# Modulation as columns, pair by pair, with the first row chunk normalised and multiplied in step with it

## The chip, the cores and the metric

The kernel runs on one NeuronCore of a Trainium2 chip. The metric is device time in microseconds, the median of several executions. One further execution was taken by the hardware profiler, and every row below comes from it. The engines are PE (TensorE: MATMUL, with its weight loads shown apart as PEld), DVE (VectorE), ACT (ScalarE), POOL (GpSimd) and SP (SyncE, which here only issues DMAs).

## What is computed

Two layers of a diffusion backbone over 1152 tokens of width 1024 (1024 sample tokens, 128 prompt tokens). Of a layer only its entry matters here:

```
mod_ctx = silu(c_ctx) @ w_mod[l] + b_mod[l]      # (3072,)
mod_lat = silu(c)     @ w_mod[l] + b_mod[l]
shift, scale, gate = split(mod, 3)
xn = rmsnorm(h, norm_g) * (1.0 + scale) + shift
a_in, a_z, b_in, b_z, q_lat, kv_lat, k_rope, c_z, g_all = split(xn @ w_in)
```

After it come the Fourier, pooling and attention branches, their gates, and the output projection with its residual.

## The kernel before, in words

Each engine has a program of its own, and semaphores join them. What follows is layer 0, up to the end of its token-major products.

**Modulation.** The shift and scale parts of `w_mod[0]` come as 16 units of 128 columns (`raw`, four slots of 128x8x128 floats, 512 KB a unit; unit n takes the slot of unit n-4 and so waits for its last use, `load_units`, L518). `mod_item` (L1562) multiplies a unit with PE: for each of 8 blocks of the contraction the stationary operand is `silu_c` (128x2, two conditions) and the unit's block moves past it, 128 columns. The result is a row pair, 2x128, which DVE copies to `mod_flat` (L1220). In the trace each float32 product is two weight loads and two matmuls, so an item is 16 of each. When all 16 are copied, 16 small transposes (L1591) turn them into columns, one DVE instruction adds the bias (L1222), and `scales` (L1208) forms the factors.

**Normalising.** The 9 row tiles of 128 tokens go in three chunks of 384 tokens. ACT squares and sums a tile (L700), takes the root (L705), DVE scales the rows (L1153, `xhat`). Then for each of 8 feature blocks f: three PE transposes (`norm_turn`, L1579, into PSUM banks 6 and 7), ACT applies scale and shift (`norm_values`, L718), DVE rounds to the high part (L1172), and the low part is a subtraction on POOL for even f (L987) and on DVE for odd f (L1175). ACT may be three blocks ahead of the low parts.

**Weights of the products.** Six units of `w_in` ("tok" 0 to 5) are split into high and low parts, ACT first (L685), POOL second (L980). Units 0 and 1 serve the products of kind p=0 (256 columns), units 2 to 5 those of kind p=1 (416 columns).

**Token-major products.** For p=0 and then p=1, for each of the 9 tiles, 8 blocks of three matmuls (`three_pass`, L1552 to L1554) into banks 0 to 2. ACT reads each result out (L750 for p=0, L753 and L754 for p=1). The turns of chunks 1 and 2 stand between the matmuls of tiles 1 and 4 of p=0. After the 18 tile products the feature-major products begin.

**Order.** SP issues six units, then a row tile and three units, three times over, then the rest of the units up to "tok" 1, three constants, and the later rows and units. All of layer 0's modulation stands ahead of the first turn on PE and ahead of the first value on ACT.

Of the kernel before, what the change touches and what calls it, by code (L numbers as in the profile page):

```python
# [107 lines left out]
def bank_plan():  # L108
# [48 lines left out]
NORM_IN_OUT = {5: (0, 0, 3), 6: (0, 3, 6), 7: (0, 6, 8)}  # L157
NORM_IN_ROWS = {1: 1, 4: 2}

# [102 lines left out]
def hybrid_step(nc, x_prompt, x_sample, cache_ckv, cache_krope, c, c_ctx, norm_g, w_mod, b_mod, w_in,  # L262
# [124 lines left out]
    vec_rows = r.put("vec_rows", [P])  # L387
    mod_flat = r.put("mod_flat", [16, P])

# [54 lines left out]
    def wcols(w, l, c0, width=P):  # L444
        return w[l].rearrange("(k p) n -> p k n", p=P)[:, :, c0:c0 + width]
    for m in range(16):
        unit(("mod", 0, m), [(0, KF, wcols(w_mod, 0, m * P))], None, (0, "mod", m))
    for l in range(DEPTH):
        for u, (c0, width) in enumerate(TOK_UNITS):
            split_unit(("tok", l, u), [(0, KF, wcols(w_in, l, c0, width))], 2 + u if u < 2 else 4 + u,  # L450
                       (l, "tok", (TT if u < 2 else 2 * TT) - 1))
        last_in[0] = (l, "tok", 2 * TT - 1)
# [104 lines left out]
    def _(sp):  # L557
# [13 lines left out]

        load_units(sp, 0, 6)
        for t in range(CT):
            load_rows(t)
            load_units(sp, 6 + 3 * t, 9 + 3 * t)
        load_units(sp, 15, unit_at[("tok", 0, 2)])
        for dst, src in ((q_scale, "q_scale"), (edge, "edge"), (pool_mat, "vec_zero")):
            sp.dma_start(dst[:], tab[src]).then_inc(S("const_in"), 16)
        for t in range(CT, 2 * CT):
            load_rows(t)  # L580
        load_units(sp, unit_at[("tok", 0, 2)], unit_at[("tok", 0, 4)])
        for t in range(2 * CT, TT):
            load_rows(t)
        for l in range(DEPTH):

            for ch in range(NCH):
                low_done(sp, KF * ((l * NCH) + ch + 1))
                sl = slice(ch * CH, (ch + 1) * CH)
                sp.dma_start(park_hi[:, :, sl], XH[:, :, sl].bitcast(F32)).then_inc(S("parked"), 16)
                sp.dma_start(park_lo[:, :, sl], XL[:, :, sl].bitcast(F32)).then_inc(S("parked"), 16)  # L590
                if ch == 0:
                    load_units(sp, unit_at[("tok", l, 4)], unit_at[("tok", l, 5)] + 1)
# [82 lines left out]
    def _(act):  # L675
# [31 lines left out]
        def norm_values(l, ch, f0, f1):  # L707

            for f in range(f0, f1):
                n = ch * KF + f  # L710
                b = filled(act, l, "norm", n)
                if n + l * NCH * KF >= 3:
                    low_done(act, l * NCH * KF + n - 2)
                if f == 0:
                    act.wait_ge(S("scale_ready"), l + 1)
# [18 lines left out]
        for l in range(DEPTH):  # L734

            filled(act, l, "norm", KF - 1)
            squares(l, 1)
            roots(l, 1)
            squares(l, 2, PS[:, 3:5, :].rearrange("p b n -> p (b n)"))
            roots(l, 2)  # L740
            for p in range(2):
                for t in range(TT):
                    b = filled(act, l, "tok", p * TT + t)
                    if t == 0:
                        act.wait_ge(S("xhat"), 9 * l + (9 if p else 3))
                        if l:
                            for ch in ((1, 2) if p else (0,)):
                                act.wait_ge(S(f"mid_out{ch}"), 16 * CT)
                    if p == 0:
                        ins = a.activation(atok[:, t, :], PS[:, b, 0:256], ACT.Copy)  # L750
                    else:
                        s = t if t < 8 else 9
                        a.activation(qlat[:, t, :], PS[:, b, 0:QR], ACT.Copy)  # L753
                        ins = a.activation(kvk[:, s, 0:LATENT - QR], PS[:, b, QR:LATENT], ACT.Copy)  # L754
                    ins.then_inc(bank_free[b], 1)
                    if p == 0 and t + 1 in NORM_IN_ROWS:
                        norm_values(l, NORM_IN_ROWS[t + 1], 0, KF)
                    if p == 0 and t in (2, 5):
                        for u in ((2, 3) if t == 2 else (4, 5)):
                            split_high(("tok", l, u))  # L760
                    if p == 1 and t in (3, 5):
                        split_high(("feat", l, t // 5))
            if l:
# [207 lines left out]
    def _(pool):  # L971
# [10 lines left out]
        def norm_low(l, ch, f0=0, f1=KF):  # L982
            for f in range(f0 + f0 % 2, f1, 2):
# [4 lines left out]
                                ALU.subtract).then_inc(S("xn_low_even"), 1)  # L988

        split_low(("tok", 0, 0))  # L990
        norm_low(0, 0, 0, 4)
        split_low(("tok", 0, 1))
        norm_low(0, 0, 4, KF)
        for l in range(DEPTH):
            for u in range(2, 6):
                if u % 2 == 0:
                    norm_low(l, u // 2)
                split_low(("tok", l, u))
            split_low(("feat", l, 0))
            split_low(("feat", l, 1))  # L1000
# [139 lines left out]
    def _(dve):  # L1140
# [73 lines left out]
        read_out(dve, 0, "vec", 0)  # L1214
        for m in range(16):
            if m == 10:
                norm_factors(0, 0)
                norm_rows(0)
            b = filled(dve, 0, "mod", m)
            v.tensor_copy(mod_flat[0:2, m, :], PS[0:2, b, 0:P]).then_inc(bank_free[b], 1)  # L1220
        b = filled(dve, 0, "modt", 0)
        v.tensor_tensor(modT[:, 0, 0:16, :], PS[:, b, 0:32].rearrange("p (m c) -> p m c", c=2),  # L1222
                        vecT[:, 0:16].unsqueeze(2).broadcast_to([P, 16, 2]), ALU.add).then_inc(bank_free[b], 1)
        read_out(dve, 0, "modt", 0)
        scales(0)
        norm_dve(0, 0)

        for l in range(DEPTH):

            norm_factors(l, 1)  # L1230
            norm_rows(1)
            norm_factors(l, 2)
            norm_dve(l, 1)
            norm_rows(2)
# [4 lines left out]
            for t in range(TT):  # L1239
                s = t if t < 8 else 9  # L1240
                read_out(dve, l, "tok", TT + t)
                squares = rot_tmp[:].rearrange("p a b -> p (a b)")
# [304 lines left out]
    def _(pe):  # L1547
# [7 lines left out]

        def mod_item(m):

            b = pe_takes(pe, 0, "mod", m)
            nu = unit_at[("mod", 0, m)]
# [25 lines left out]
        pe.wait_ge(S("silu_c"), 2)  # L1585
        for m in range(16):
            mod_item(m)
        for m in range(10, 16):
            read_out(pe, 0, "mod", m)
        for m in range(16):  # L1590
            ins = nc.tensor.transpose(PS[:, 6, 2 * m:2 * m + 2], mod_flat[0:2, m, :], ident[0:2, 0:2])  # L1591
        ins.then_inc(bank_full[6], 1)
        norm_turn(0, 0, 0, KF)

        for l in range(DEPTH):

            for p in range(2):
                pe.wait_ge(S("split_low"), split_k[("tok", l, 5 if p else 1)] + 1)
                for t in range(TT):
                    if p == 0 and t % CT == 0:  # L1600
                        low_done(pe, KF * (l * NCH + t // CT + 1))
                    b = pe_takes(pe, l, "tok", p * TT + t)
                    sl = slice(t * P, (t + 1) * P)
                    out = PS[:, b, 0:LATENT if p else 256]
                    for k in range(KF):
                        wh, wl = (wlat[:, i, k, :] if p else bs[:, 0:2, i, k, :] for i in range(2))
                        if p == 0 and t in NORM_IN_ROWS:
                            norm_turn(l, NORM_IN_ROWS[t], k, k + 1)
                        ins = three_pass(out, XH[:, k, sl], XL[:, k, sl], wh, wl, k == 0, k == KF - 1)
                    ins.then_inc(bank_full[b], 1)  # L1610

# [276 lines left out]
```

## Time and profile before

| | us |
|---|---|
| median of 3 runs | 2243.26 (2242.95 to 2243.73) |
| the profiled execution | 2243.49 |
| its span on the core | 2241.4 |
| PE busy | 2159.3 |
| DVE, ACT, POOL busy | 1088.0, 880.8, 650.6 |
| last read-out of a token-major product of layer 0 begins | 136.65 |

The span is the stretch that the profiler covers, and the profiled execution's own time is 2.1 us above it. A busy share is an average over the span. The change touches only the first part, so the stretches up to the last read-out are the ones to read.

### The profile page before, as it was taken

The page shows a single profiled execution, that of the slowest core. Times are in us where ns is not written, and L with a number is a line of the kernel's source. Part 1 is how long each engine was busy: PE and PEld are TensorE (multiplying, and loading weights), DVE is VectorE, ACT ScalarE, POOL GpSimd, SP SyncE. Part 2 cuts the span into 40 slices and gives each one's busy share as a digit, 9 for nine tenths or more (in the row PEclk, how much of TensorE's full clock was granted, in tenths as well). Part 3 has the DMA queues.
Part 4 walks back from the last instruction along what each step waited for, and adds up shares of the span by engine and source line. Part 5 has one row for each costly group of instructions (what it writes and reads, how often), then busy time and mean ns, then how long its engine had stood idle before and what let it go on. Part 6 is the DMA issues. An engine that isn't in the chain of part 4 may idle for free.

```text
span 2241.4 us, 36176 instructions
## 1 busy us (share of the span) xinstructions
PE 2159.3 (96%) x13453; PEld 2016.8 (90%) x13453; DVE 1088.0 (49%) x2773; ACT 880.8 (39%) x2203; POOL 650.6 (29%) x574
## 2 busy tenths in 40 slices
PE   6999999999989999999999999999999999999997
PEld 4999878878889999999989997778878999999997
DVE  3440368888845667663152314888886111120313
ACT  2421257777831212113152213777777112111312
POOL 1223022322321234333441321222323213343252
PEclk9999999999999999999999999999999999999999
DMA  9710000000343333224255100000005111111132
GB/s 286 255 34 25 26 1 1 1 1 1 120 145 92 94 83 99 72 66 135 68 201 169 33 8 25 1 1 2 1 2 202 48 36 48 42 50 42 45 132 85
DMA packets 194623, 155.69 MB, mean 69 GB/s; under 512 B 8637, under 2 KB 186001, under 8 KB 193425
## 3 DMA queue, kind: packets, MB, share of 16 engines
q1 hardware_dynamic: 194448, 153.38, 22.3%
q8 instruction: 108, 1.77, 0.3%
q14 instruction: 67, 0.54, 0.1%
HBM read 124.89 MB, written 28.48 MB: 68 GB/s over the span
## 4 chain that ended last, share of the span: by engine, by line
PE 84%; DVE 6%; ACT 4%; issue 3%; DMA 1%; SPq 0%; POOL 0%; DVEq 0%; POOLq 0%; ACTq 0%
PE ps L1552 22%; PE ps L1554 22%; PE ps L1553 22%; PE ps L1732 4%; PE ps L1686 3%; PE ps L1757 3%; PE ps L1758 2%; PE ps L1689 2%; DVE partmax L1399 1%; DVE kT L1369 1%; DVE probsT L1412 1%; DMA raw<-in_w_mod 1%; PE ps L1562 1%; ACT kT L857 1%; PE ps L1660 1%
## 5 line engine op out<-in xcount | busy, mean ns | idle before, releaser
L1552 PE MATMUL ps<-xn_high,split_ws 128*128 128x384 f32 x1488 | 499.6, 336 | 0.0
L1554 PE MATMUL ps<-xn_high,split_ws 128*128 128x384 f32 x1488 | 497.3, 334 | 0.0
L1553 PE MATMUL ps<-xn_low,split_ws 128*128 128x384 f32 x1488 | 497.1, 334 | 0.0
L938 ACT ACTIVATE sigmoids<-ps 128x384 f32<-128x384 f32 x144 | 70.5, 492 | 620.3 <-PE ps L1554 620.3
L1553 PEld LDWEIGHTS ps<-xn_low,split_ws 128*128 128x128 f32 x1488 | 279.5, 188 | 0.0
L1552 PEld LDWEIGHTS ps<-xn_high,split_ws 128*128 128x128 f32 x1488 | 279.4, 188 | 0.0
L1554 PEld LDWEIGHTS ps<-xn_high,split_ws 128*128 128x128 f32 x1488 | 279.3, 188 | 0.0
L1412 DVE TENSOR_TENSOR probsT<-ps,probsT 128x384 fp32r<-128x384 f32 x384 | 213.3, 555 | 70.6 <-ACT sum_inv_rows L833 41.1
L810 ACT ACTIVATE probs<-ps,negmax 128x384 f32<-128x384 f32 (+1 forms) x400 | 229.7, 575 | 20.0 <-DVE negmax L1405 19.5
L826 ACT ACTIVATE probsT<-ps 128x384 fp32r<-128x384 f32 x384 | 188.8, 492 | 83.3 <-PE ps L1732 52.3
L1732 PE MATMUL ps<-ident,probs 128*128 128x128 f32 x1168 | 198.0, 277 | 18.7 <-DVE kT L1369 15.0
L1399 DVE TENSOR_REDUCE partmax<-ps 128x1 f32<-128x384 f32 (+1 forms) x400 | 212.4, 535 | 1.7 <-PE ps L1554 1.3
L980 POOL TENSOR_TENSOR split_ws<-raw,split_ws 128x1024 fp32r<-128x1024 f32 x66 | 158.9, 2409 | 163.4 <-ACT split_ws L685 163.4
L1732 PEld LDWEIGHTS ps<-ident,probs 128*128 128x128 f32 x1168 | 132.4, 140 | 81.6 <-issue 74.6
L1489 DVE TENSOR_TENSOR products<-ps,sigmoids 128x384 f32<-128x384 f32 x96 | 53.5, 557 | 293.0 <-PE ps L1554 240.3
L1107 POOL TENSOR_TENSOR merged<-merged,products 128x384 f32<-128x384 f32 x90 | 92.3, 1026 | 334.7 <-DVE products L1489 333.9
L1757 PE MATMUL ps<-probsT,head_values 128*128 128x256 f32 x576 | 156.2, 291 | 12.4 <-DVE mixed_out L1433 12.4
L1552 PE MATMUL ps<-kT,qT 128*128 128x384 f32 (+1 forms) x400 | 163.2, 408 | 1.0 <-ACT probs L810 1.0
L1069 POOL TENSOR_TENSOR branch<-mixed_out,branch 64x256 f32<-64x256 f32 (+1 forms) x80 | 54.3, 679 | 338.8 <-DVE mixed_out L1433 337.9
L1758 PE MATMUL ps<-probsT,head_values 128*128 128x256 f32 x576 | 150.6, 281 | 0.0
L1554 PE MATMUL ps<-kT,qT 128*128 128x384 f32 (+1 forms) x400 | 134.1, 335 | 0.0
L1553 PE MATMUL ps<-kT,qT 128*128 128x384 f32 (+1 forms) x400 | 133.3, 333 | 0.0
(222 smaller groups left out, 4577.5 us busy)
## 6 DMA issues: line engine op xcount, KB each, us to landing
raw<-in_w_in SPq DMA_DIRECT2D x74, 512.0 KB, 4.0
raw<-in_w_mod SPq DMA_DIRECT2D x48, 512.0 KB, 5.2
park_high<-xn_high SPq DMA_DIRECT2D x6, 1536.0 KB, 6.7
park_low<-xn_low SPq DMA_DIRECT2D x6, 1536.0 KB, 10.6
xn_high<-park_high SPq DMA_DIRECT2D x2, 4608.0 KB, 16.2
rows<-in_x_sample SPq DMA_DIRECT2D x16, 512.0 KB, 6.7
raw<-in_w_out SPq DMA_DIRECT2D x16, 512.0 KB, 6.9
rows_mid<-rows SPq DMA_DIRECT2D x9, 512.0 KB, 2.6
```

The lines of the kernel that those rows point to most:

```text
L810: a.activation((P0, P1)[m % 2][:, c * CH:c * CH + w], PS[:, b, 0:w], ACT.Exp, bias=negmax[:, m % 2:m % 2 + 1], accum_out=partsum[:, m % 2, ...
L826: ins = a.activation(turned_place(m, gg, 0), PS[:, b, 0:n * P].rearrange("p (k c) -> p k c", k=n), ACT.Copy)
L980: g.tensor_tensor(d[:, 1], raw_unit(n), d[:, 0].bitcast(F32), ALU.subtract).then_inc(S("split_low"), 1)
L1107: g.tensor_tensor(Y[:, u % KF, sl], Y[:, u % KF, sl], prod[:, q % 2, :], ALU.add).then_inc(S("y_sum"), 1)
L1399: v.tensor_reduce(partmax[:, m % 2, c:c + 1], PS[:, b, 0:w], AX.X, ALU.max).then_inc(S("partmax"), 1)
L1412: v.tensor_tensor(turned_place(m, gg, 1), PS[:, b, 0:n * P].rearrange("p (k c) -> p k c", k=n), turned_place(m, gg, 0).bitcast(F32), ALU.s ...
L1552: mm(out, wh, xh, start=first, stop=False)
L1553: mm(out, wh, xl, start=False, stop=False)
L1554: return mm(out, wl, xh, start=False, stop=last)
L1732: ins = nc.tensor.transpose(PS[:, b, q * P:(q + 1) * P], (P0, P1)[m % 2][:, (3 * gg + q) * P:(3 * gg + q + 1) * P], ident[:])
L1757: mm(PS[:, b, 0:w], vhl, xh, start=(kt == 0 or gr == 4), stop=False)
L1758: ins = mm(PS[:, b, 0:w], vhl, xl, start=False, stop=last)
```

## The change

The kernel's text changes in five places.

- **Operands.** `mod_item` makes the unit's 128x128 block the stationary operand and lets the two columns of `silu_c` move, so that the result is a column pair, 128x2. DVE adds the bias from PSUM straight into `modT`. `mod_flat`, the 16 small transposes and `scales(0)` go.
- **Order of the items.** `MODS` takes shift f and scale f together. After each pair DVE forms the scale of block f, and `scale_ready` counts blocks.
- **Chunk 0 beside it.** From pair 3 on PE makes turns of chunk 0 behind the pairs (`TURN_IN_MODS`), and steps of the three p=0 tiles of chunk 0, block by block (`TOK_IN_MODS`, `tok_step`), with all three tiles open in banks 0 to 2. Chunk 1 follows in the same manner, two blocks behind its turns. The items have banks 3 to 5 instead of 0 to 5.
- **Order of the tiles.** In layer 0 three tiles of p=1 come after the six tiles of p=0, with the turns of chunk 2 in the second of them (`TOK_ORDER`, `NORM_IN_TOK`).
- **Loads.** The rows of chunk 0 come behind units 0 and 1 and behind units 2 and 3; "tok" 0 stands behind item 5 and "tok" 1 behind item 7 in the chain of slots. "tok" 2 to 5 come before the rows of chunk 2, the constants last.

```diff
-    add(0, "mod", 0, 6, 16)
-    add(0, "modt", 6, 1, 1)
+    add(0, "mod", 3, 3, 16)
...
+NORM_IN_TOK = ({(1, 1): 2}, {(0, 1): 1, (0, 4): 2})
+MODS = [m for f in range(KF) for m in (f, KF + f)]
+TOK_ORDER = ([(0, t) for t in range(2 * CT)] + [(1, t) for t in range(CT)] + [(0, t) for t in range(2 * CT, TT)]
+             + [(1, t) for t in range(CT, TT)],
...
+TURN_IN_MODS = {3: (0, 1), 4: (2, 3), 5: (4, 5), 6: (6,), 7: (7,)}
+TOK_IN_MODS = {5: (0,), 6: (1, 2), 7: (3, 4, 5, 6, 7)}
+DVE_IN_MODS = {3: (0,), 4: (1, 2), 5: (3, 4), 6: (5, 6), 7: (7,)}
...
+    for i, m in enumerate(MODS):
+        unit(("mod", 0, m), [(0, KF, wcols(w_mod, 0, m * P))], None, (0, "mod", i))
+        if i in (5, 7):
+            tok_unit(0, (i - 5) // 2)
...
+        load_units(sp, 0, 2)
+        load_rows(0)
+        load_rows(1)
+        load_units(sp, 2, 4)
+        load_rows(2)
+        load_units(sp, 4, unit_at[("tok", 0, 2)])
+        for t in range(CT, 2 * CT):
             load_rows(t)
+        load_units(sp, unit_at[("tok", 0, 2)], unit_at[("tok", 0, 5)] + 1)
+        for t in range(2 * CT, TT):
+            load_rows(t)
...
+                if l == 0 and ch == 0:
+                    act.wait_ge(S("scale_ready"), f + 1)
...
+        norm_values(0, 0, 0, 2)
         split_high(("tok", 0, 0))
-        norm_values(0, 0, 0, 4)
         split_high(("tok", 0, 1))
-        norm_values(0, 0, 4, KF)
+        norm_values(0, 0, 2, KF)
...
+            if l == 0:
+                for t in range(CT):
+                    tok_rows(0, t)
+                split_high(("tok", 0, 2))
+                split_high(("tok", 0, 3))
+                norm_values(0, 1, 0, KF)
+                split_high(("tok", 0, 4))
+                split_high(("tok", 0, 5))
+            squares(l, 2, beside_squares)
             roots(l, 2)
...
+        norm_low(0, 0, 0, 2)
         split_low(("tok", 0, 0))
-        norm_low(0, 0, 0, 4)
         split_low(("tok", 0, 1))
-        norm_low(0, 0, 4, KF)
+        norm_low(0, 0, 2, KF)
         for l in range(DEPTH):
             for u in range(2, 6):
-                if u % 2 == 0:
+                if l and u % 2 == 0:
                     norm_low(l, u // 2)
                 split_low(("tok", l, u))
+                if l == 0 and u % 2:
+                    norm_low(l, u // 2)
...
-                ins = mm(PS[0:2, b, 0:P], silu_c[:, k, :], raw[:, nu % 4, k, :], start=(k == 0), stop=(k == KF - 1))
+                ins = mm(PS[:, b, 0:2], raw[:, nu % 4, k, :], silu_c[:, k, :], start=(k == 0), stop=(k == KF - 1))
...
+        def tok_step(ch, k):
+
+            low_done(pe, KF * ch + k + 1)
+            for t in range(ch * CT, (ch + 1) * CT):
+                n = tok_item(0, 0, t)
+                b = pe_takes(pe, 0, "tok", n) if k == 0 else item(0, "tok", n)[0]
+                sl = slice(t * P, (t + 1) * P)
+                ins = three_pass(PS[:, b, 0:256], XH[:, k, sl], XL[:, k, sl], bs[:, 0:2, 0, k, :], bs[:, 0:2, 1, k, :],
+                                 k == 0, k == KF - 1)
+                if k == KF - 1:
+                    ins.then_inc(bank_full[b], 1)
+
+        for f in range(KF):
+            mod_item(2 * f)
+            mod_item(2 * f + 1)
+            for ff in TURN_IN_MODS.get(f, ()):
+                norm_turn(0, 0, ff, ff + 1)
+            for k in TOK_IN_MODS.get(f, ()):
+                if k == 0:
+                    pe.wait_ge(S("split_low"), split_k[("tok", 0, 1)] + 1)
+                tok_step(0, k)
+        for k in range(KF + 2):
+            if k < KF:
+                norm_turn(0, 1, k, k + 1)
+            if k >= 2:
+                tok_step(1, k - 2)
```

On PE, at the seam from the modulation to the first products, the program before has all items, the small transposes, all eight turns of chunk 0 and then tile 0:

```order
L1562 MATMUL ps<-raw,silu_c 2x128 x128
L1591 MATMUL ps<-ident,mod_flat 128x2 x16
L1579 MATMUL ps<-ident,xhat 128x128 x24
L1552 MATMUL ps<-split_br,xn_high 128x256
L1553 MATMUL ps<-split_br,xn_high 128x256
```

On PE, in the changed program, item 7, the turns of blocks 0 and 1, pair 4 (items 8 and 9) and the turn of block 2 read so; the output is now 128x2 and `raw` the stationary operand:

```order
L1599 MATMUL ps<-silu_c,raw 128x2 [waits raw_in0,bank_free4]
L1599 MATMUL ps<-silu_c,raw 128x2 x7
L1616 MATMUL ps<-ident,xhat 128x128 [waits bank_free6,xhat]
L1616 MATMUL ps<-ident,xhat 128x128 x5
L1599 MATMUL ps<-silu_c,raw 128x2 [waits raw_in2,bank_free5]
L1599 MATMUL ps<-silu_c,raw 128x2 x7
L1599 MATMUL ps<-silu_c,raw 128x2 [waits raw_in3,bank_free3]
L1599 MATMUL ps<-silu_c,raw 128x2 x7
L1616 MATMUL ps<-ident,xhat 128x128 [waits bank_free6]
L1616 MATMUL ps<-ident,xhat 128x128 x2
```

The turns of chunk 0 moved from behind all items to between them, beginning behind item 7.

On SP, in the DMA queue of the changed program from item 4's unit on, the units' loads and what each waits for:

```order
L533 DMA raw<-in_w_mod 128x8x128 [waits bank_full3]
L533 DMA raw<-in_w_mod 128x8x128 [waits bank_full4]
L533 DMA raw<-in_w_in 128x8x128 [waits bank_full5]
L533 DMA raw<-in_w_mod 128x8x128 [waits bank_full3]
L533 DMA raw<-in_w_mod 128x8x128 [waits bank_full4]
L533 DMA raw<-in_w_in 128x8x128 [waits bank_full5]
L533 DMA raw<-in_w_mod 128x8x128 [waits split_low]
L533 DMA raw<-in_w_mod 128x8x128 [waits bank_full3]
L533 DMA raw<-in_w_mod 128x8x128 [waits bank_full4]
L533 DMA raw<-in_w_mod 128x8x128 [waits split_low]
```

Item 8's unit (the seventh row, the first that waits for `split_low`) now stands behind the splitting of "tok" 0; before, every modulation unit waited for a PE product alone.

On ACT, in the changed program, between the two roots of chunks 1 and 2:

```order
L721 ACTIVATE root<-ssq 128x3 [waits mean_sq]
L762 ACTIVATE fourier_in<-ps 128x256 [waits xhat,bank_full0]
L762 ACTIVATE fourier_in<-ps 128x256 [waits bank_full1]
L762 ACTIVATE fourier_in<-ps 128x256 [waits bank_full2]
L701 ACTIVATE split_latent<-raw 128x8x128 [waits raw_in2]
L701 ACTIVATE split_latent<-raw 128x8x128 [waits raw_in3]
L736 ACTIVATE xn_value<-ps,modT,scaleT 128x384 [waits xn_low_odd,xn_low_even,bank_full6]
```

Before, the root of chunk 1 had only the squares of chunk 2 between itself and the root of chunk 2; the read-outs, the splits and all values of chunk 1 moved in between.

## Rows read from the trace of the kernel before

**Rows 1.** Page, busy us (share of the span) and instructions.
```profile
PE 2159.3 (96%) x13453; PEld 2016.8 (90%) x13453; DVE 1088.0 (49%) x2773; ACT 880.8 (39%) x2203; POOL 650.6 (29%) x574
```

**Rows 2.** Stretches: us, busy of PE, PEld, DVE, ACT, POOL, clock, DMA share, GB/s.
```profile
20.00:40.00 20.00, 16.26 (x146) 11.64 (x144) 3.52 (x10) 4.71 (x8) 0.00 (x0) 1.00 1.14 305
40.00:60.00 20.00, 11.89 (x76) 9.41 (x74) 14.71 (x26) 11.85 (x20) 9.05 (x6) 0.66 0.94 314
...
90.00:100.00 10.00, 10.00 (x73) 9.96 (x72) 0.00 (x0) 1.16 (x3) 1.69 (x2) 1.00 1.06 325
```

**Rows 3.** Waits of PE, 0 to 220 us: total, times, longest.
```profile
PE ps L1562 <- DMA raw<-in_w_mod: 6.2, 4, 2.5
...
PE ps L1552 <- DVE xn_low L1175: 5.0, 1, 5.0
```

**Rows 4.** Timeline, modulation items: start us, us, engine, what, count [idle before].
```profile
7.61 12.83 PE L1562 MATMUL ps<-raw,silu_c 128*2 128x128 f32 x96 [2.48 <-DMA raw<-in_w_mod]
11.29 0.28 DVE L1220 COPY mod_flat<-ps 2x128 f32<-2x128 f32 x1 [5.88 <-PE ps L1562]
...
35.14 7.15 PE L1562 MATMUL ps<-raw,silu_c 128*2 128x128 f32 x64 [1.26 <-DMA raw<-in_w_mod]
```

**Rows 5.** Weight loads by form (stationary width after the star), busy us, mean ns.
```profile
L1562 PEld LDWEIGHTS ps<-raw,silu_c 128*2 128x2 f32 x256 | 22.1, 88 | 15.0 <-issue 7.5
...
L1689 PEld LDWEIGHTS ps<-ckvT,wkv 128*64 128x64 f32 x96 | 9.3, 135 | 10.6 <-DVE kT L1369 3.0 <-ACT spectrum L799 1.4 <-issue 0.5
...
L1707 PEld LDWEIGHTS ps<-spectrum,chan_dft 128*128 128x128 f32 x32 | 5.2, 192 | 1.9 <-issue 1.9
```

**Rows 6.** Timeline of PE, single matmuls whose starts give the spacing.
```profile
57.57 0.42 PE L1554 MATMUL ps<-split_br,xn_low 128*128 128x256 f32 x1
57.78 0.41 PE L1552 MATMUL ps<-split_br,xn_high 128*128 128x256 f32 x1
...
337.09 0.28 PE L1553 MATMUL ps<-kT,qT 128*128 128x128 f32 x1
337.21 0.28 PE L1554 MATMUL ps<-kT,qT 128*128 128x128 f32 x1
```

**Rows 7.** Timeline of PE, small transposes and turns (three per turn).
```profile
42.76 1.12 PE L1591 MATMUL ps<-ident,mod_flat 2*128 2x2 f32 x16 [0.46 <-DVE mod_flat L1220]
...
64.10 0.49 PE L1579 MATMUL ps<-ident,xhat 128*128 128x128 f32 x3
...
64.79 0.49 PE L1579 MATMUL ps<-ident,xhat 128*128 128x128 f32 x3
```

**Rows 8.** Stretches of PE alone: us, busy, granted clock, DMA share, GB/s.
```profile
44.00:46.00 2.00, 0.85 (x6) 1.00 1.02 363
48.00:50.00 2.00, 1.68 (x7) 0.50 1.08 350
60.00:61.00 1.00, 1.00 (x11) 1.00 1.04 372
```

**Rows 9.** Timeline and chain: one value, two splits, a first load, a square.
```profile
3.44 4.03 DMA raw<-in_w_mod
...
42.19 1.06 ACT L685 ACTIVATE split_br<-raw 128x1024 fp32r<-128x1024 f32 x1 [4.22 <-DMA raw<-in_w_in]
43.33 2.35 POOL L980 TENSOR_TENSOR split_br<-raw,split_br 128x1024 fp32r<-128x1024 f32 x1 [42.88 <-ACT split_br L685]
...
51.35 0.67 ACT L718 ACTIVATE xn_value<-ps,modT,scaleT 128x384 f32<-128x384 f32 x1 [0.38 <-PE ps L1579]
...
58.51 1.03 ACT L700 ACTIVATE ps<-rows 128x1024 f32<-128x1024 f32 x1
```

**Rows 10.** Timeline of ACT, read-outs of tile products.
```profile
92.95 0.38 ACT L750 ACTIVATE fourier_in<-ps 128x256 f32<-128x256 f32 x1 [2.50 <-PE ps L1554]
95.83 0.39 ACT L750 ACTIVATE fourier_in<-ps 128x256 f32<-128x256 f32 x1 [2.50 <-PE ps L1554]
...
132.12 0.39 ACT L753 ACTIVATE qlat<-ps 128x256 f32<-128x256 f32 x1 [3.96 <-PE ps L1554]
136.65 0.39 ACT L753 ACTIVATE qlat<-ps 128x256 f32<-128x256 f32 x1 [3.96 <-PE ps L1554]
```

More of the change, by code:

```diff
@@ L728, in _, with tok_rows @@
         roots(0, 0)
+        norm_values(0, 0, 0, 2)
         split_high(("tok", 0, 0))
-        norm_values(0, 0, 0, 4)
         split_high(("tok", 0, 1))
-        norm_values(0, 0, 4, KF)
+        norm_values(0, 0, 2, KF)
         for l in range(DEPTH):
+            def tok_rows(p, t):
+                b = filled(act, l, "tok", tok_item(l, p, t))
+                if t % CT == 0:
+                    act.wait_ge(S("xhat"), 9 * l + (3 if p == 0 else 6 if l == 0 and t == 0 else 9))
+                if l and t == 0:
+                    for ch in ((1, 2) if p else (0,)):
+                        act.wait_ge(S(f"mid_out{ch}"), 16 * CT)
+                if p == 0:
+                    ins = a.activation(atok[:, t, :], PS[:, b, 0:256], ACT.Copy)
+                else:
+                    s = t if t < 8 else 9
+                    a.activation(qlat[:, t, :], PS[:, b, 0:QR], ACT.Copy)
+                    ins = a.activation(kvk[:, s, 0:LATENT - QR], PS[:, b, QR:LATENT], ACT.Copy)
+                ins.then_inc(bank_free[b], 1)
+            beside_squares = PS[:, 3:5, :].rearrange("p b n -> p (b n)")
             filled(act, l, "norm", KF - 1)
@@ L738, in _ @@
             roots(l, 1)
-            squares(l, 2, PS[:, 3:5, :].rearrange("p b n -> p (b n)"))
-            roots(l, 2)
[L741 to L762, printed above, removed]
+            if l == 0:
[7 more added lines that the diff above has]
+            squares(l, 2, beside_squares)
+            roots(l, 2)
+            for p, t in TOK_ORDER[l][CT if l == 0 else 0:]:
+                tok_rows(p, t)
+                if (p, t + 1) in NORM_IN_TOK[l]:
+                    norm_values(l, NORM_IN_TOK[l][p, t + 1], 0, KF)
+                if l and p == 0 and t in (2, 5):
+                    for u in ((2, 3) if t == 2 else (4, 5)):
+                        split_high(("tok", l, u))
+                if p == 1 and t in (3, 5):
+                    split_high(("feat", l, t // 5))
             if l:
@@ L1214, in _ @@
         read_out(dve, 0, "vec", 0)
-        for m in range(16):
-            if m == 10:
+        for f in range(KF):
+            if f == 3:
                 norm_factors(0, 0)
                 norm_rows(0)
[L1219 to L1226, printed above, removed]
+            for i in (2 * f, 2 * f + 1):
+                m = MODS[i]
+                b = filled(dve, 0, "mod", i)
+                v.tensor_tensor(modT[:, 0, m, :], PS[:, b, 0:2], vecT[:, m:m + 1].broadcast_to([P, 2]), ALU.add)\
+                    .then_inc(bank_free[b], 1)
+            read_out(dve, 0, "mod", 2 * f + 1)
+            v.tensor_scalar(scaleT[:, f, :], modT[:, 0, KF + f, :], 1.0, vecT[:, 48 + f:49 + f], ALU.add, ALU.mult)\
+                .then_inc(S("scale_ready"), 1)
+            for ff in DVE_IN_MODS.get(f, ()):
+                norm_dve(0, 0, ff, ff + 1)
         for l in range(DEPTH):
@@ L1231, in _ @@
             norm_rows(1)
-            norm_factors(l, 2)
-            norm_dve(l, 1)
+            if l == 0:
+                norm_dve(l, 1)
+                norm_factors(l, 2)
+            else:
+                norm_factors(l, 2)
+                norm_dve(l, 1)
             norm_rows(2)
@@ L1240, in _ @@
                 s = t if t < 8 else 9
-                read_out(dve, l, "tok", TT + t)
+                read_out(dve, l, "tok", tok_item(l, 1, t))
                 squares = rot_tmp[:].rearrange("p a b -> p (a b)")
@@ L1585, in _ @@
         pe.wait_ge(S("silu_c"), 2)
[L1586 to L1593, printed above, removed]
-        for l in range(DEPTH):
[L1597 to L1610, printed above, removed]
@@ new lines, in _ @@
+        for f in range(KF):
+            mod_item(2 * f)
[11 more added lines that the diff above has]
+                tok_step(1, k - 2)
@@ new lines, in _ @@
+        for l in range(DEPTH):
+            for p, t in TOK_ORDER[l][2 * CT if l == 0 else 0:]:
+                if t == 0:
+                    pe.wait_ge(S("split_low"), split_k[("tok", l, 5 if p else 1)] + 1)
+                if p == 0 and t % CT == 0:
+                    low_done(pe, KF * (l * NCH + t // CT + 1))
+                n = tok_item(l, p, t)
+                b = pe_takes(pe, l, "tok", n)
+                sl = slice(t * P, (t + 1) * P)
+                out = PS[:, b, 0:LATENT if p else 256]
+                for k in range(KF):
+                    wh, wl = (wlat[:, i, k, :] if p else bs[:, 0:2, i, k, :] for i in range(2))
+                    if (p, t) in NORM_IN_TOK[l]:
+                        norm_turn(l, NORM_IN_TOK[l][p, t], k, k + 1)
+                    ins = three_pass(out, XH[:, k, sl], XL[:, k, sl], wh, wl, k == 0, k == KF - 1)
+                ins.then_inc(bank_full[b], 1)
```

37 lines of the change are left out of this document (15 added, 22 removed).

## The prediction

> **What bounds the kernel now.** The busy shares come first [rows 1]: PE is busy for 96% of the span, so a change pays only where PE stands idle, waits or runs at half clock. The stretches come second [rows 2]. From 90 us on PE is full at full clock; in 20 to 60 us it is busy 28.2 of 40 us, and in 40 to 60 us the granted clock averages 0.66. DMA moves 305 to 314 GB/s there, a busy share of about one, so the start is also near what the DMA queues give. The waits come third [rows 3]: PE waits 6.2 us for modulation units and 5.0 us for the first normalised chunk; the latter is what the change is to cover. Last, the read-outs give a mark [rows 10]: the final token-major product of layer 0 is read at 136.65. Everything between 95.83 and there is PE back to back, 4.53 us a tile (136.65 - 132.12), and the p=0 tiles take 2.88 (95.83 - 92.95). What stands behind the mark is unchanged and follows PE, so I move the whole time by the shift of this mark, one for one.
>
> **The operands.** An item was 16 matmuls of 128 moving columns against two-column weights. At full clock four items take 7.15 us, 1.79 each; the first item, from 7.61 until its read-out at 11.29, takes 3.7 us, half the speed [rows 4]. Now it is 16 loads of 128x128 float32 weights with two moving columns each. The trace has no such pair, so I bound it. A load of 2, 64 and 128 columns is recorded with 88, 135 and 192 ns [rows 5], so 126 more columns cost about 104 ns of load; I assume that one load doesn't overlap the next. The nearest row for a stream bound by such loads is the 128-column high/low product: its starts are 0.12 apart [rows 6], no less than the 2.88/24 = 0.12 of 256 columns [rows 10], so half the streaming bought nothing and the load set the pace. By it an item costs 16 x 0.12 = 1.9; by the slope alone 16 x 0.107 = 1.7. The lower bound is the small transposes, whose stationary operand is also 128 wide and whose moving operand has two columns: 16 in 1.12 us [rows 7], 0.07 each, 1.1 an item; but those are transposes over two partitions. I take 1.75 at full clock, nearest to the load rows: nothing is gained on PE by the swap. At half clock starts are 0.21 apart (57.57 to 57.78) [rows 6], so an item costs 3.4. The removed small transposes (1.12), the bias and the scales (0.2 and 1.6 on DVE) lay on the path once and save about 3 us; the 24 small DVE instructions in their place lie beside PE.
>
> The Trainium skill ("TensorE: Matmul & The Clock Gate", section "LDWEIGHTS (loading the stationary operand)") says that a load takes its number of columns divided by 1.2, in nanoseconds, whatever the contraction. That would be 107 ns and 1.7 us an item; the slope of the rows agrees, the small transposes don't.
>
> **The clock.** This is the dear term. While the old items streamed, in 20 to 40 us, PE kept full clock [rows 2] through pauses such as the 1.26 ahead of 35.14 [rows 4]. In 44 to 46 us it had 0.85 us of turns behind the 16 two-column transposes, and in 48 to 50 it had half clock although it was busy 1.68 of 2 us with turns; it had full clock again in 60 to 61, three microseconds into the wide products [rows 7, 8]. So work that is mostly loads and turns neither held nor regained the clock here, and the new modulation consists of just that. The engine starts at half clock as well [rows 4]. I take half clock from the first item until wide products run in a row.
>
> The same page of the Trainium skill (section "Part 4: PE-mode transpose") says that transposes don't count as work for the clock as matmuls do. The trace agrees as far as the row of 48 to 50 us goes; on loads with two moving columns no page speaks.
>
> **The queue.** Item 8's unit now waits until POOL has split "tok" 0. That stands behind the first two turns (behind item 7), two values (0.67 each), the high split (1.06), the low split (2.35) and then a first load from an empty queue (4.03) [rows 9]. With 1.1 of turns at half clock that is 1.1 + 1.3 + 1.1 + 2.4 + 4.0 = 9.9 us in which PE has no item and, behind what is in flight, DMA runs dry. SP is in order, so all later units and rows wait too. Before, no unit waited for anything but a product.
>
> **The sum, in times of the trace.** Items 0 to 7: 7.6 + 8 x 3.4 = 34.8. First load of item 8: + 9.9 = 44.7. Then eight items, 27.2; six turns at half clock, a full-clock turn being 0.69 (64.79 - 64.10) less its three products 0.36, so 0.33 [rows 7] and 0.66 now, 4.0; three steps of nine products, 27 x 0.21 = 5.7: 81.6. The steps of blocks 1 and 2 are 4 us of wide products in a row and may bring the clock back for the last two items, -3.3: 78.3. Blocks 3 to 7 are 45 products, 5.4 at full and 9.6 at half clock; I take 7: 85.3. Beside this ACT squares chunk 1 (3 x 1.03), so its rows are ready by then. Chunk 1: POOL splits "tok" 2 and 3 ahead of its low parts, and ACT's high split stands behind the read-outs: 1 + 2 x 2.4 + 1 = 6.8 with little for PE, then 72 products and the five turns left, 8.6 + 1.7, and 3 for another spell of half clock: 105.4. The first p=1 tile needs bank 0, and ACT reads tile 3 only behind two high splits (1.4), three squares (3.5) and a root: PE waits 2.4 of it, 107.8. From there 9 p=1 tiles (40.8), three p=0 tiles (8.6), eight turns (2.6): 159.8. The mark was at 136.65, so the change costs 23 us. Against the profiled execution's 2243.5 that is 2266.5; the median stands 0.2 below that execution, so 2266. The unknown half-clock spells give 2259 to 2281.
>
> **The rivals.**
> - **The clock comes back during the items (2250).** If the continuous loads count as work, the clock is full from the second item or so, is lost in the 9 us without an item, and costs two items again. Items 0 to 7 end near 29.5 (units come at 1.79, rows between), item 8 starts at 38.7, eight items at 1.8, two of them at 3.4, with turns and three steps of 3.2: 61.5. Then 5.4, the 20 us of chunk 1, 2.4 and 52.0: 141.5 to 145, 5 to 8 us slower, 2248 to 2252. For it: the old items held the clock through their pauses [rows 2, 4]. Against: the rows of 44 to 50.
> - **Short loads, half clock (2255).** If a load costs 0.07 as in the small transposes, an item is 2.2 at half clock. Sixteen items lose 19 us less than above, but units arrive at 1.79 and the last items pay fully for the clock; the mark falls near 148, 12 slower.
> - **Faster (2237).** Short loads and full clock from item 8 on: an item takes 1.1, less than its unit's 1.79, and DMA is the bound. Items 0 to 7 end at 27 as the units arrive, the last unit is there by 50, and turns and steps 0 to 4 hide between. Block 7 ends at 55 where before the first product began at 57.0; 20 + 2.4 + 52 more give 130, 6.5 faster. The place is the sixteen loads per item; it decides from an item below 1.79 at the clock then granted.
> - **No difference (2243).** The pause at item 8 is shorter, or the earlier chunk 0 gives back exactly what the items lose; also the case in which PE is not held by the splitting of "tok" 2 and 3.
>
> **How the numbers follow.** Half clock throughout with full-length loads: 0.43. Clock back in between: 0.26. Short loads at half clock: 0.12. Faster: 0.10. No difference: 0.09. A measurement of this kernel tells about 0.2%, 4.5 us, from no change, so the bounds are 2238.8 and 2247.8. Of the second case a tenth falls within them, and of the faster case a quarter: faster 0.08, same 0.14, slower 0.78. The range that leaves out about 2 in 10 goes from 2241 to 2278: below it lies the faster case, above it the first case with all its slow spells and items of 1.9.
>
> **What would show it.** Right: a weight load of the new form recorded near 190 ns; items 3.4 us apart; granted clock 0.5 in the stretches up to 70 us; PE idle for 8 to 10 us behind item 7, released by DMA, and SP waiting there for POOL's `split_br`; ACT reading tile 3 behind the squares of chunk 2. The last qlat read-out near 160. Wrong: items of 1.1 to 1.8 with clock 1.0, DMA above 300 GB/s without a hole, or a mark below 137. If the mark and the total move by different amounts, the one-for-one step fails.

## The result and the profile after

The changed kernel takes 2266.06 us (median of 4 runs, 2263.89 to 2271.4) against 2243.11 (4 runs, 2242.81 to 2243.73) for the kernel before on the same chip: ratio 1.0105 [1.0088, 1.0123]. It is 1% slower. The forecast was 2266, the range 2241 to 2278. The profiled execution took 2271.4, the longest of the four, with a span of 2269.3, so its positions may lie a few microseconds behind those of a typical run.

PE's timeline, the modulation items and the first turns (start us, us, engine and line, operation, count, and in brackets the idle time before and what ended it), to be set beside [rows 4, 7]:

```profile
7.71 27.44 PE L1599 MATMUL ps<-silu_c,raw 128*128 128x2 f32 x128 [2.75 <-DMA raw<-in_w_mod]
35.02 1.52 PE L1616 MATMUL ps<-ident,xhat 128*128 128x128 f32 x6
44.69 6.96 PE L1599 MATMUL ps<-silu_c,raw 128*128 128x2 f32 x32 [8.16 <-DMA raw<-in_w_mod]
...
52.82 6.83 PE L1599 MATMUL ps<-silu_c,raw 128*128 128x2 f32 x32
...
62.75 6.82 PE L1599 MATMUL ps<-silu_c,raw 128*128 128x2 f32 x32
...
69.96 0.56 PE L1589 MATMUL ps<-split_br,xn_high 128*128 128x256 f32 x1
...
73.95 4.01 PE L1599 MATMUL ps<-silu_c,raw 128*128 128x2 f32 x32
```

Eight items take 27.4 us, 3.4 each. Then PE stands 8.2 us without work, and six more items come at 3.4. Only the last two are quicker, 3.9 for both (73.95 to 77.81), behind four microseconds of wide products (69.96 to 73.95).

The pause in the other engines' timelines (SPq is SP's DMA queue):

```profile
35.93 1.31 ACT L736 ACTIVATE xn_value<-ps,modT,scaleT 128x384 f32<-128x384 f32 x2 [6.84 <-PE ps L1616]
37.15 1.99 ACT L701 ACTIVATE split_br<-raw 128x1024 fp32r<-128x1024 f32 x2
...
37.08 1.00 POOL L1016 TENSOR_TENSOR xn_low<-xn_value,xn_high 128x384 fp32r<-128x384 f32 x1 [36.64 <-DVE xn_high L1203]
38.27 4.64 POOL L1009 TENSOR_TENSOR split_br<-raw,split_br 128x1024 fp32r<-128x1024 f32 x2 [0.19 <-ACT split_br L701]
...
40.64 19.41 SPq L533 DMA_DIRECT2D raw<-in_w_mod  x8
```

Two values end at 37.2, ACT's first high split at 38.2, POOL's first low split at 40.6; there SP issues item 8's unit, and it lands 4 us later. Meanwhile the DMA engines of this core move nothing for 9 us (us, busy of PE with instructions, granted clock, DMA share, GB/s):

```profile
32.00:41.00 9.00, 4.54 (x21) 1.00 0.00 0
```

The waits of SP and PE say the same (us in total, times, longest):

```profile
SPq L533 <- POOL split_br L1009: 11.9, 1, 11.9
...
PE ps L1599 <- DMA raw<-in_w_mod: 10.9, 2, 8.2
...
PE ps L1589 <- POOL xn_low L1016: 3.7, 1, 3.7
PE ps L1589 <- ACT fourier_in L762: 3.0, 1, 3.0
PE ps L1616 <- ACT xn_value L736: 2.1, 1, 2.1
```

The wait of 5.0 us for the first normalised chunk [rows 3] is gone, as the change meant; 8.2 for item 8 and 8.8 behind chunk 0 have come. Two sets of stretches in the same columns as above:

```profile
8.00:62.00 54.00, 54.00 (x254) 1.00 0.71 209
```

is of the kernel with the new operands alone (below), and these are of the change:

```profile
38.00:44.00 6.00, 0.00 (x0) 1.00 0.35 104
...
78.00:82.00 4.00, 4.00 (x23) 0.57 1.07 305
...
88.00:98.00 10.00, 6.16 (x28) 0.52 0.77 288
...
108.00:112.00 4.00, 3.21 (x10) 0.61 1.03 372
```

A trap in reading: the clock column shows 1.00 from 8 to 62 us, while the starts stand 0.213 apart there, twice what they are at full clock. The column seems to be right only from the first change of clock that the trace has recorded. Until then the spacing of equal instructions tells the clock. From 78 us on the column and the spacing agree, and the clock is lost three more times. The last read-out, the mark of [rows 10]:

```profile
162.95 0.39 ACT L765 ACTIVATE qlat<-ps 128x256 f32<-128x256 f32 x1 [3.96 <-PE ps L1591]
```

The mark moved by 26.3, the span by 27.9.

### The profile page after: what moved, and what is told of

Same layout as the page of the kernel before. It is cut to its first block, busy times and chain, and to the rows that moved or that the text cites. A ratio compares the mean times of both kernels' runs of the same rounds, so it can differ in the third digit from the quotient of the medians.

```text
span 2269.3 us, 36173 instructions
## 1 busy us (share of the span) xinstructions
PE 2185.7 (96%) x13437; PEld 2053.6 (90%) x13437; DVE 1081.6 (48%) x2778; ACT 879.6 (39%) x2203; POOL 649.9 (29%) x574
## 4 chain that ended last, share of the span: by engine, by line
PE 85%; DVE 6%; ACT 4%; issue 3%; DMA 1%; POOL 0%; DVEq 0%; SPq 0%; POOLq 0%; ACTq 0%
PE ps L1589 22%; PE ps L1591 21%; PE ps L1590 21%; PE ps L1788 4%; PE ps L1813 3%; PE ps L1742 3%; PE ps L1814 2%; PE ps L1599 2%; PE ps L1745 2%; DVE partmax L1436 1%; DVE kT L1406 1%; DVE probsT L1449 1%; ACT kT L886 1%; PE ps L1716 1%; PE ps L1831 1%
```

## The experiments

| kernel | us, median (lowest to highest, runs) | ratio to before | mark |
|---|---|---|---|
| change | 2266.06 (2263.89 to 2271.4, 4) | 1.0105 [1.0088, 1.0123] | 162.95 |
| e1 new operands alone | 2262.13 (2261.23 to 2263.02, 4) | 1.0080 [1.0065, 1.0095] | 153.68 |
| e2 change, old operands | 2253.58 (2251.89 to 2253.95, 4) | 1.0041 [1.0026, 1.0056] | 146.94 |
| e3 change, splits first | 2261.55 (2256.92 to 2263.43, 4) | 1.0075 [1.0059, 1.0090] | 155.19 |
| e4 both | 2243.26 (2241.38 to 2243.99, 10) | 0.9995 [0.9985, 1.0004] | 136.13 |
| e5 e4, queues interleaved | 2239.59 (2237.35 to 2242.11, 11) | 0.9983 [0.9974, 0.9992] | 132.71 |

Each ratio is to the kernel before as it ran beside that kernel; its medians were 2243.11 beside the change, 2244.30 beside e1 to e4 and 2243.65 beside e5. The mark is that of the profiled execution.

The first theory was that the operands cost the clock (some 17 us) and the queue a pause (some 9), and that the two add up to the loss. The rival was that the moved order as such costs, whatever the operands.

**e1, the new operands alone.** Order, loads and turns are those of the kernel before.

```diff
-                ins = mm(PS[0:2, b, 0:P], silu_c[:, k, :], raw[:, nu % 4, k, :], start=(k == 0), stop=(k == KF - 1))
+                ins = mm(PS[:, b, 0:2], raw[:, nu % 4, k, :], silu_c[:, k, :], start=(k == 0), stop=(k == KF - 1))
...
-        for m in range(16):
-            ins = nc.tensor.transpose(PS[:, 6, 2 * m:2 * m + 2], mod_flat[0:2, m, :], ident[0:2, 0:2])
```

> The program before with the new operands alone: the unit's 128x128 block is stationary, two columns move, DVE adds the bias from PSUM; the small transposes go, the order, the queue and the loads stay. Theory A (the operands cost, because a stream of loads with two moving columns runs at half clock): in the profile of the change 32 loads at half clock took 6.9 us, two items, so the 16 items end at 7.6 + 16 x 3.43 = 62.5 where they ended at 42.3 before; the small transposes and scales give back 1 us, and the first products, which began 12 us behind the last item, begin with it later. The mark (last qlat read-out, 136.65 before) goes to 155, the time to 2261 (2257 to 2264). Theory B (the new order and queue cost, not the operands): the items take what they took, the mark falls by 1 us, 2242.

17.8 us slower. The items are one block on PE's timeline:

```profile
7.83 54.75 PE L1560 MATMUL ps<-silu_c,raw 128*128 128x2 f32 x256 [2.85 <-DMA raw<-in_w_mod]
```

54.75 / 16 = 3.42 for each, without a pause, to the end. Before, the last items ended at 35.14 + 7.15 = 42.3 [rows 4]. That is 20.3 later. From there to the first product of tile 0 it takes 11.9 in e1 (62.58 to 74.48) and took 14.7 before (42.29 to 57.00), because the small transposes are gone and the two instructions of `scales`, which stay, take 0.24 in place of 1.63. So the first product comes 17.5 later, and the mark moved by 17.0.

**e2, the change with the old operands.** `silu_c` is stationary again, DVE copies the row pairs, and two small transposes follow each pair; they take one of the items' three banks.

```diff
-                ins = mm(PS[:, b, 0:2], raw[:, nu % 4, k, :], silu_c[:, k, :], start=(k == 0), stop=(k == KF - 1))
+                ins = mm(PS[0:2, b, 0:P], silu_c[:, k, :], raw[:, nu % 4, k, :], start=(k == 0), stop=(k == KF - 1))
...
+            for i in (2 * f, 2 * f + 1):
+                read_out(pe, 0, "mod", i)
+                ins = nc.tensor.transpose(PS[:, b, 2 * (i % 2):2 * (i % 2) + 2], mod_flat[0:2, i, :], ident[0:2, 0:2])
```

> The changed program with the old operands in the modulation: silu_c is stationary and the unit's 128 columns move, DVE copies the row pair, two small transposes a pair turn it (bank 5), DVE adds the bias; order, queue and loads are the changed ones. Theory A (the operands and the clock cost): items 0 to 7 end near 28 instead of 35, the 8 to 9 us without an item at item 8 stay, since the queue is unchanged, and items 8 to 15 stream at 1.8 once the clock is back, 14 to 19 us instead of 24 plus steps; the mark goes from 163 to 142 or 145: 2248 to 2252. Theory B (the order and the queue cost): 2263 to 2267 as in the change.

9.3 us slower than before, 12.5 faster than the change and 1.6 above the range of theory A. PE's timeline has full-clock pairs and the pause:

```profile
18.86 3.71 PE L1604 MATMUL ps<-raw,silu_c 128*2 128x128 f32 x32 [0.61 <-DMA raw<-in_w_mod]
...
38.66 5.78 PE L1604 MATMUL ps<-raw,silu_c 128*2 128x128 f32 x32 [8.51 <-DMA raw<-in_w_mod]
...
45.77 3.65 PE L1604 MATMUL ps<-raw,silu_c 128*2 128x128 f32 x32
```

The pause is 8.5 here too, so it belongs to the queue and not to the operands. The pair behind it takes 2.1 more: the idle time lost the clock as well. The two parts alone, 17.8 and 9.3, add to 27.1, the change costs 23.0. A small part of the 9.3 is the price of e2's own transposes: PE waits for their copies eight times, 1.8 us in all.

**e3, the splits ahead of the values.** ACT splits "tok" 0 before the root and "tok" 1 behind it, POOL both before any low part. Nothing else differs from the change.

```diff
         squares(0, 0)
-        roots(0, 0)
-        norm_values(0, 0, 0, 2)
         split_high(("tok", 0, 0))
+        roots(0, 0)
         split_high(("tok", 0, 1))
-        norm_values(0, 0, 2, KF)
+        norm_values(0, 0, 0, KF)
```

> The changed program, but ACT splits tok 0 ahead of the root of chunk 0 and tok 1 behind it, ahead of all values, and POOL makes both low splits ahead of its first low part. Nothing else. If the 8.2 us that PE waits for item 8's unit come from the split standing behind turns and values, they go, and nothing later takes their place as long as items take 3.4: 2258 (2256 to 2260). If the queue itself were short of time there (units landing late anyway), less than 3 us go: 2263 or more. Item times stay 3.43 in both.

The pause is gone, and by the medians only 4.5 us come back (5.7 with each kernel set against the kernel before beside it). That is outside both ranges, and the four runs lie between 2256.92 and 2263.43. On PE's timeline:

```profile
35.07 1.52 PE L1614 MATMUL ps<-ident,xhat 128*128 128x128 f32 x6
36.39 6.83 PE L1597 MATMUL ps<-silu_c,raw 128*128 128x2 f32 x32
...
61.52 0.56 PE L1587 MATMUL ps<-split_br,xn_high 128*128 128x256 f32 x1
...
65.51 6.82 PE L1597 MATMUL ps<-silu_c,raw 128*128 128x2 f32 x32
```

The last pair starts 8.4 earlier than in the change (73.95 there), but it now runs at half clock, 6.8 in place of 3.9, so it ends 5.5 earlier. The same four microseconds of wide products stand ahead of it (61.52 to 65.51); why they brought the clock back in the one execution and not in the other stays open. Further on the clock favours e3, whose first p=1 tile has full clock, so that its mark comes 7.8 earlier and its profiled execution takes 8.0 less, which is nearly the whole pause. The medians' smaller gain is therefore not explained by the last pair, and with four runs that spread over 7 us on each side it is uncertain.

**e4, both.** e2 with the edit of e3.

> Both edits at once: old operands in the modulation, in the changed order, and the splits of tok 0 and 1 first. Theory A: no pause at item 8 and items that stream at full clock at the pace of the units, so the last item ends near 50, the first tiles near 56, and the mark near 132 to 134: 2238 to 2241, below the kernel before. The gain over e2 is then 10 us, more than the 8 us of the pause, since the clock isn't lost in it. Theory B (order and queue cost): no better than e3, 2258.

10.3 faster than e2, as theory A said of the gain, and the time of the kernel before to within the interval, which is 2 above its range of 2238 to 2241. The operands and the pause are therefore the whole loss; the rival, that the order as such costs, has nothing left. But the order brings nothing either. Where its gain went, PE's waits of e4 to 220 us show:

```profile
PE ps L1602 <- DMA raw<-in_w_mod: 5.8, 5, 2.6
...
PE ps L1592 <- POOL xn_low L1017: 3.8, 1, 3.8
PE ps L1592 <- ACT fourier_in L763: 3.0, 1, 3.0
```

The wait for chunk 0 [rows 3] has become a wait for chunk 1's low parts, which POOL makes behind the splits of "tok" 2 and 3, and one for tile 3's read-out, which ACT makes behind the squares of chunk 2.

**e5, these two queues interleaved.** POOL makes a low part between splits, ACT reads tiles 3 to 5 before the squares, and the last p=0 tiles come one p=1 tile later.

```diff
+                norm_low(0, 1, 0, 2)
+                split_low(("tok", 0, 2))
+                norm_low(0, 1, 2, 4)
+                split_low(("tok", 0, 3))
+                norm_low(0, 1, 4, KF)
...
+                for t in range(CT, 2 * CT):
+                    tok_rows(0, t)
             squares(l, 2, beside_squares)
```

> e4 (old operands in the changed order, splits of tok 0 and 1 first) with the two waits behind chunk 0 taken apart: POOL makes a low part of chunk 1, then the split of tok 2, then the next low part, then tok 3, and ACT its high splits between the values likewise; ACT reads tiles 3 to 5 out ahead of the squares of chunk 2; the turns of chunk 2 go one tile later and the last three p=0 tiles behind four p=1 tiles instead of three. In e4 PE waited 3.8 us for the first low part of chunk 1 and 3.0 us for the read-out of tile 3, and lost the clock in 60 to 72 us. If these waits are what is left (theory A), both go and the spell of half clock shortens: 6 to 9 us less, the mark near 128 to 130, 2234 to 2238, faster than the kernel before. If POOL's work or the loads set the pace of chunk 1 (theory B), the time stays within 3 us of e4: 2240 to 2244.

3.7 faster than e4 (3.0 with each set against the kernel before beside it) and 4.1 faster than before: 0.9983 [0.9974, 0.9992], the only version ahead of the kernel before, and by little. The gain lies between the two theories, and the edits to POOL, ACT and the order of the tiles weren't tried apart. The wait for the read-out is gone from PE's list and the other is shorter:

```profile
PE ps L1603 <- POOL xn_low L1021: 3.3, 2, 2.4
...
PE ps L1603 <- POOL split_latent L1014: 1.1, 1, 1.1
```

The waits that are left are 2.4 shorter in sum, and the mark came 3.4 earlier; the clock was higher too, but how the gain divides between the two isn't shown. The stretches 60 to 80 and 80 to 100 us, of e4 first and then of e5 (busy of PE, PEld, DVE, ACT, POOL, clock, DMA share, GB/s):

```profile
60.00:80.00 20.00, 14.56 (x96) 13.79 (x94) 8.52 (x12) 9.30 (x16) 11.19 (x8) 0.74 0.52 192
80.00:100.00 20.00, 18.04 (x96) 17.13 (x97) 9.71 (x17) 10.06 (x26) 4.83 (x5) 0.91 0.41 149
```

```profile
60.00:80.00 20.00, 15.22 (x96) 14.31 (x96) 8.45 (x12) 9.98 (x16) 11.91 (x8) 0.83 0.58 211
80.00:100.00 20.00, 19.95 (x114) 19.12 (x115) 9.70 (x17) 11.48 (x29) 4.30 (x4) 1.00 0.35 125
```

**e6 to e10, is it the clock?** Spacing alone can't tell a half clock from a load that takes 0.21 us at any clock. These kernels are e1 with unread work ahead of each item: four, eight and twelve products of 128x128 weights with 128 moving columns (two matmuls each), or sixteen transposes of the identity.

```diff
+            for _ in range(4):
+                mm(PS[:, b, 256:384], ident[:], ident[:], start=True, stop=True)
...
+            for _ in range(16):
+                nc.tensor.transpose(PS[:, b, 256:384], ident[:], ident[:])
```

> e1 (columns alone) with four further 128x128 products of 128 moving columns ahead of each item, written beside its result and never read: more work, 0.87 us an item at full clock and 1.7 at half. If the half clock comes from streams of loads with hardly a moving column (theory A) and this share of wide work is enough to hold the clock, an item is 1.98 + 0.87 = 2.85 instead of 3.43 and the last ends near 54 instead of 62.5: about 2254, 8 us faster than e1 although it does more. If the half clock has another cause, or the share is too small, an item is 3.43 + 1.7 = 5.2 and the time 28 us above e1: 2290.

> As e6 with eight such products an item, 1.75 us at full clock. Theory A: an item is 3.73 at full clock, the last ends near 68, 2266 to 2268. If the clock stays at half: an item is 3.43 + 3.4 = 6.9 and the time 2316.

> As e7, with sixteen transposes of the identity an item in place of the eight products: the same time on PE at full clock (16 x 0.11 = 1.75). If transposes hold the clock as products do, the same as e7, 2266 to 2268; if they don't, an item is 6.9 and the time 2316. The trace of the kernel before, which had half clock while it was busy with turns at 48 to 50 us, speaks for the second.

> Before with the new operands, and in each item twelve products of 128x128 weights with 128 moving columns more, which nobody reads. With eight, the same program ran in 2267 or in 2316. Theory: the clock follows how much of an item is moving columns, and with twelve it is granted from an early item on, in every run. A product is two matmuls of 0.11 at full clock, so an item is 1.98 + 2.7 = 4.7, the sixteen end near 82, that is 20 behind the 62.5 of the new operands alone at half clock: 2281 to 2285 in all runs. Rival 1, the clock isn't had at all while such loads are in the stream, whatever is added: 3.4 + 5.3 = 8.7 an item, 2344 to 2348. Rival 2, as with eight products, chance decides: both values, or some between.

> The kernel with eight more products per item once more, to have a trace of each of its two times. In the short kind (2267) the items should stand 1.98 + 1.8 = 3.8 apart from an early one on, which would be the price of the new item at full clock; in the long kind 6.83 apart as seen. Rival: in the short kind it is something other than the clock of the items, and their distance is 6.83 as well.

| added to each item | runs, us | items apart |
|---|---|---|
| nothing (e1) | 2261.23 to 2263.02, 4 runs | 3.42 |
| 4 products (e6) | 2289.38 to 2289.99, 4 runs | 5.12 |
| 8 products (e7) | 2315.92, 2267.13, 2266.66, 2316.15 | 6.83 |
| 8 products (e10) | 2315.56, 2315.88, 2316.28 | 6.83 |
| 16 transposes (e8) | 2294.68, 2268.67, 2308.83, 2271.8 | 6.72, from 72.68 on 3.49 |
| 12 products (e9) | 2280.62, 2280.73, 2279.64 | 4.47 |

The kernel with most work in its items is faster than e6 and than every long run of e7, e8 and e10. PE's timeline of e9 and, behind it, of e7, each an early item:

```profile
7.59 5.35 PE L1560 MATMUL ps<-ident 128*128 128x128 f32 x24 [2.44 <-DMA raw<-in_w_mod]
12.78 1.84 PE L1562 MATMUL ps<-silu_c,raw 128*128 128x2 f32 x16
14.49 2.92 PE L1560 MATMUL ps<-ident 128*128 128x128 f32 x24
17.25 1.84 PE L1562 MATMUL ps<-silu_c,raw 128*128 128x2 f32 x16
```

```profile
14.44 3.76 PE L1560 MATMUL ps<-ident 128*128 128x128 f32 x16
17.99 3.41 PE L1562 MATMUL ps<-silu_c,raw 128*128 128x2 f32 x16
21.27 3.76 PE L1560 MATMUL ps<-ident 128*128 128x128 f32 x16
```

The same item takes 14.49 - 12.78 = 1.71 in e9 and 21.27 - 17.99 = 3.28 in e7. The weight loads of the items (busy us, mean ns), e9 and then e7:

```profile
L1562 PEld LDWEIGHTS ps<-silu_c,raw 128*128 128x128 f32 x256 | 29.9, 192 | 0.0
```

```profile
L1562 PEld LDWEIGHTS ps<-silu_c,raw 128*128 128x128 f32 x256 | 56.5, 333 | 0.0
```

So the price was the clock, and not the load: e1's items took 54.75 where sixteen at full clock are 27.4, before any wait for a unit. My expectation for e9 was right in kind (full clock from the first item's loads on, and three runs alike) and 0.2 an item too high, so that the time came out 0.4 under its range.

Between the ends the same program ran in either time. e7 and e10 are one program: five of its seven runs took 2316, two 2267. No trace of a short run was obtained, so that the short ones had full clock in the items is argued: one item at half clock (6.8) from 7.6 and fifteen at 1.71 + 1.84 = 3.55 end near 67.7, 5.1 behind e1's 62.6, and 2262.1 + 5.1 = 2267.2 is close to the 2267.13 and 2266.66 that were measured.

Sixteen transposes did no less than eight products. In e8's profile the clock came back in the middle of nothing but transposes and loads:

```profile
64.59 3.41 PE L1562 MATMUL ps<-silu_c,raw 128*128 128x2 f32 x16
67.86 3.27 PE L1560 MATMUL ps<-ident 128*128 128x128 f32 x16
...
72.68 1.94 PE L1560 MATMUL ps<-ident 128*128 128x128 f32 x16
74.46 1.84 PE L1562 MATMUL ps<-silu_c,raw 128*128 128x2 f32 x16
```

## Why the prediction was right, and where it was not

| step | forecast | the change |
|---|---|---|
| items 0 to 7 end | 34.8 | 35.0 |
| item 8 starts | 44.7 | 44.7 |
| last item ends | 78.3 | 77.8 |
| chunk 0 multiplied | 85.3 | 85.1 |
| chunk 1 multiplied | 105.4 | 105.8 |
| first p=1 tile starts | 107.8 | 108.8 |
| mark | 159.8 | 163.0 |
| time | 2266 | 2266.06 (profiled run 2271.4) |

**The clock.** The dear term held: half clock from the first item until wide products came in a row, then full for the last pair. e1 shows it alone, e9 shows that the clock was the cause. The 3.3 given back for the last pair came true in the profiled execution, but not in e3 behind the same wide products, so that term was right partly by luck.

**The item's price.** I took 1.75 at full clock between 1.1 and 1.9, from the load rows, and 3.4 at half; measured are 1.71 (e9) and 3.42 (e1). The slope of the load rows gives 0.106 a load, where I wrote 0.107; the item is 1.7 by either. The load was the bound, as the 128-column product said [rows 6], and the 0.07 of the small transposes [rows 7] was no guide. The load is recorded with 192 ns at full clock, as the row of that form said [rows 5]. But the sign that I named, near 190 in the change, came out wrong: most of its items ran at half clock, where the record is 333 (e1).

**The queue.** The chain of splits took what was summed: 44.69 - 35.02 = 9.7 against 9.9, of which PE was without work for 8.2. e2 shows the same pause with other operands, e3 and e4 remove it with the edit that the chain names. Its worth was 10.3 with the old operands. With the new it was 4.5 by the medians and 8.0 between the two profiled executions; which is nearer the truth is open.

**The sign in the clock column failed.** I expected 0.5 up to 70 us and the column says 1.00. The step itself was right, its sign was not: [rows 4] already had a first item at half speed, and the column of that trace says 1.00 for its first 20 us.

**Behind chunk 1.** The wait for tile 3's read-out was 3.0 against 2.4, and the first p=1 tile began at half clock, 0.35 apart:

```profile
108.79 0.61 PE L1589 MATMUL ps<-split_latent,xn_high 128*128 128x416 f32 x1 [2.96 <-ACT fourier_in L762]
109.20 0.55 PE L1590 MATMUL ps<-split_latent,xn_high 128*128 128x416 f32 x1
109.55 0.55 PE L1591 MATMUL ps<-split_latent,xn_low 128*128 128x416 f32 x1
```

From there to the mark it took 54.2 and not the 52.0 of the sum, which was all at full clock. In e3 the same tile began at full clock, and from there to its mark at 155.19 it took 52.6:

```profile
102.58 0.42 PE L1587 MATMUL ps<-split_latent,xn_high 128*128 128x416 f32 x1 [2.96 <-ACT fourier_in L761]
```

So 1.6 of the 2.2 are the half clock, which I had left out of the last term after counting it in the earlier ones, and 0.6 the sum itself.

**One for one** held to 1.6 us in the change and to 2.7 in e1. Span less mark is 2104.8 before, 2106.3 in the change, 2107.4 in e1, 2104.8 in e2, 2106.2 in e3, 2104.7 in e5: it wanders, and what decides it stays open.

**The hit on 2266.0 is partly luck.** The profiled run, by whose kind of times the sum was made, took 2271.4, 5 above the sum; the other three lie 4.9 to 7.5 below that run. The kernel before spreads over 0.9 us in four runs (over 3.8 in the thirteen beside e1 to e4), the change over 7.5. That the clock's coming and going in its first 110 us makes this spread is likely by e7, e8 and the last pair of e3, but no two traces of the change were compared.

**The rivals.** Clock back during the items: no, 14 of 16 ran at half clock, and the two others are those that the forecast excepted. Short loads: no, 1.71. Faster: no. No difference: no, only e4, with old operands and the splits first, took the time of before.

## What to carry to other kernels

Swapping operands so that the wide one is stationary leaves PE as busy as before and can still halve its clock: cost such a stream at both clocks, and read the clock off the spacing of equal instructions. When compute is moved in beside loads that recycle buffers, follow the chain that frees each buffer through every engine's order; here two values ahead of a split, and the split itself, left the DMA engines with nothing for 9 us and PE for 8. And when idle time is removed from a stretch whose clock comes and goes, don't read the gain off one place: in e3 the same edit was worth 8.4 at the start of the last pair, 5.5 at its end, 7.8 at the mark and 4.5 by the medians.

## What was not expected of the hardware

- **More work, less time.** Four unread products an item gave 2289.9, twelve gave 2280.6, and eight 2267 or 2316. The same program on the same data differs by 2.2%, which the sum behind e7 puts down to the clock of its first hundred microseconds alone.
- **Transposes count here.** The Trainium skill ("TensorE: Matmul & The Clock Gate", section "Part 4: PE-mode transpose") says that they don't, and the prediction leaned on [rows 8] for it. In e8 the clock came back at 70 us with nothing but them and the loads on PE, and two runs of four took 2269 and 2272; the loads without them (e1) took 54.75 us at half clock, and e1's four runs agree to 1.8 us. So in this kernel the measurement speaks against the page. The row of 48 to 50 us was a stretch at half clock with turns in it, no proof that turns can't hold the clock.
- **The clock column** reads 1.00 ahead of the first recorded change of clock, also where instructions take twice their time.
